# Decoder step of two layers: sample value matmuls alternate between PSUM partition groups, sample vector operations cover both samples, and the inverse subtracts half of the columns

## What is computed

```
kb_all = concat([past_k, kb]); vb_all = concat([past_v, vb])
p = softmax(q . k * 64**-0.5 + forget_bias)
o = einsum('nhqk,nkhd->nqhd', p, v)
```

```
a_mat = where(strict, einsum(kbeta, kc) * decay, 0)
t_mat = triangular_solve(eye + a_mat, eye)
```

## Time and profile before

| | us |
|---|---|
| three runs | 1669.51, 1686.29, 1686.38 |
| profiled execution | 1672.87 |
| its span | 1671.1 |
| PE, DVE busy in the span | 1406.3, 976.6 |
| ACT, POOL busy in the span | 652.9, 217.0 |
| granted PE clock, mean | 0.879 |

### The profile page before, as it was taken

One profiled execution on the slowest core, in us unless ns is written; L12 is line 12 of the kernel. 1 busy time (PEld: TensorE's weight loads), 2 busy tenths in 40 slices (PEclk: granted clock), 3 DMA queues, 4 the chain that ended last, 5 costly groups with the idle time before them and its releaser, 6 DMA issues.

```text
span 1671.1 us, 28028 instructions
## 1 busy us (share of the span) xinstructions
PE 1406.3 (84%) x9968; PEld 1273.6 (76%) x9968; DVE 976.6 (58%) x1596; ACT 652.9 (39%) x1054; POOL 217.0 (13%) x176
## 2 busy tenths in 40 slices
PE   6999979887687478999799999797867775799997
PEld 5999969865465178999799999796645543699996
DVE  4666355575554656664566644657565536566644
ACT  4654443433000245654555544333420002555543
POOL 1000020033222220000110001102231212200000
PEclk9999989957797689999989999897677875899998
DMA  6555645344351243555545646344444302345553
GB/s 212 179 177 159 174 135 169 108 129 133 122 155 54 55 135 120 180 169 158 176 134 184 192 140 189 125 141 125 130 121 144 106 27 81 109 146 181 165 167 95
DMA packets 286120, 234.16 MB, mean 140 GB/s; under 512 B 19899, under 2 KB 282019, under 8 KB 286057
## 3 DMA queue, kind: packets, MB, share of 16 engines
q1 hardware_dynamic: 286056, 233.37, 45.8%
HBM read 228.65 MB, written 5.37 MB: 140 GB/s over the span
## 4 chain that ended last, share of the span: by engine, by line
PE 77%; DVE 16%; ACT 3%; issue 3%; DMA 1%; SPq 0%; DVEq 0%; POOLq 0%; ACTq 0%
PE ps L1396 19%; PE ps L1397 18%; PE ps L1398 18%; PE ps L1591 5%; PE ps L1688 2%; DVE s L1114 1%; PE ps L1687 1%; DVE nlo L937 1%; PE ps L1540 1%; DVE yt L920 1%; PE ps L1543 1%; PE ps L1592 1%; ACT whi L591 1%; PE ps L1509 1%; DVE oms L1153 1%
## 5 line engine op out<-in xcount | busy, mean ns | idle before, releaser
L1396 PE MATMUL ps<-nhi,whi 128*128 128x264 f32 x1936 | 565.1, 292 | 66.9 <-DVE nlo L937 46.3
L1397 PE MATMUL ps<-nlo,whi 128*128 128x264 f32 x1936 | 559.6, 289 | 0.0
L1398 PE MATMUL ps<-nhi,wlo 128*128 128x264 f32 x1936 | 558.8, 289 | 0.0
L888 DVE TENSOR_TENSOR wlo<-raw,whi 128x1024 fp32r<-128x1024 f32 (+2 forms) x376 | 394.6, 1091 | 278.6 <-ACT whi L591 278.3
L1396 PEld LDWEIGHTS ps<-nhi,whi 128*128 128x128 f32 x1936 | 376.4, 194 | 73.5 <-DVE nlo L937 35.0
L591 ACT ACTIVATE whi<-raw 128x1024 fp32r<-128x1024 f32 (+2 forms) x376 | 336.8, 945 | 191.9 <-PE ps L1398 121.7
L1397 PEld LDWEIGHTS ps<-nlo,whi 128*128 128x128 f32 x1936 | 376.5, 194 | 0.2
L1398 PEld LDWEIGHTS ps<-nhi,wlo 128*128 128x128 f32 x1936 | 374.3, 193 | 0.0
L1396 PE MATMUL ps<-hhi,whi 128*128 128x264 f32 x704 | 201.6, 286 | 9.1 <-DVE hlo L905 9.1
L1398 PE MATMUL ps<-hhi,wlo 128*128 128x264 f32 x704 | 200.8, 285 | 0.0
L1397 PE MATMUL ps<-hlo,whi 128*128 128x264 f32 x704 | 200.4, 285 | 0.0
(11 more groups left out here) (337 smaller groups left out, 1645.9 us busy)
## 6 DMA issues: line engine op xcount, KB each, us to landing
raw<-in_ffn_gate_dram SPq DMA_DIRECT2D x44, 1024.0 KB, 5.3
raw<-in_ffn_up_dram SPq DMA_DIRECT2D x44, 1024.0 KB, 5.3
raw<-in_ffn_down_dram SPq DMA_DIRECT2D x64, 704.0 KB, 4.5
raw<-in_w_in_dram SPq DMA_DIRECT2D x24, 1024.0 KB, 5.6
kslot<-in_cache_fox_k_dram SPq DMA_DIRECT2D x128, 128.0 KB, 2.7
vslot<-in_cache_fox_v_dram SPq DMA_DIRECT2D x128, 128.0 KB, 2.4
raw<-in_w_out_dram SPq DMA_DIRECT2D x8, 1024.0 KB, 5.0
kslot<-in_state_swa_k_dram SPq DMA_DIRECT2D x32, 128.0 KB, 2.8
```

Of the source, the lines that this page charges most:

```text
L888: tt2(wlo[s][:, a:b], raw[s][:, a:b], whi[s][:, a:b].bitcast(F32), ALU.subtract).then_inc(S(f"w_lo{s}"), 1)
L1396: mm(out, wh, hi_, start=first, stop=False)
L1397: mm(out, wh, lo_, start=False, stop=False)
L1398: return mm(out, wl, hi_, start=False, stop=last)
```

## The change

Three edits. Line numbers move by up to 7: L1289 and L1290 are L1284 and L1285 after it, L1591 is L1590, L1150 and L1153 are L1147 to L1149.

```
-                        for i in range(2):
-                            b, u = 2 * j + i, 2 * (j % 2) + i
-                            stt(f(s13[:, u, 0:NPG, :]), f(s13[:, u, 0:NPG, :]), sc, f(bias[:, b, 0:NPG, :]), ALU.mult, ALU.add)
+                        two, own = s13[:, u:u + 2, :, :], sx[:, 2 * j:2 * j + 2, :, :]
+                        stt(f(two[:, :, 0:NPG, :]), f(two[:, :, 0:NPG, :]), sc, f(bj[:, :, 0:NPG, :]), ALU.mult, ALU.add)
...
-                            red(pmax[:, i, 0, :], s13[:, u + i, 0:FOX_PG, :].rearrange("p g h -> p h g"), AX.X, ALU.max)
+                        red(pmax[:, :, 0, :], two[:, :, 0:FOX_PG, :].rearrange("p i g h -> p i h g"), AX.X, ALU.max)
...
                     def sample_out(j):
                         dve.wait_ge(S("pv_mm"), V("pv_mm", j + 1))
-                        where = [orow(m, i) for m in range(2) for i in range(2)]
-                        for r0 in where:
-                            ins = dve.reciprocal(small[r0:r0 + H, 124:125], ps[r0:r0 + H, 7, GW:GW + 1])
-                        ch(ins)
-                        for r0 in where:
-                            ins = stt(oms[r0:r0 + H, j, :], ps[r0:r0 + H, 7, 0:GW], small[r0:r0 + H, 124:125],
-                                      const[r0:r0 + H, COL["head_block"][0]:COL["head_block"][0] + GW], ALU.mult, ALU.mult)
-                        ins.then_inc(S("oms"), 1)
+                        den = small[0:OROWS, 124:125]
+                        ch(ts(den, ps[0:OROWS, 7, GW:GW + 1], 0.5, None, ALU.max))
+                        ch(dve.reciprocal(den, den))
+                        stt(oms[:, j, :], ps[0:OROWS, 7, 0:GW], den, C("head_block", OROWS), ALU.mult, ALU.mult).then_inc(S("oms"), 1)
...
+                            part = lambda ap, side: ap.rearrange("p (c a e) -> p c a e", a=2, e=b)[:, :, side, :]
                             if k < len(LEVELS) - 1:
-                                tt2(tm[:, t, :], tm[:, t, :], ps[:, 3 * t + 1, :], ALU.subtract)
-                            tt2(tt[:, t, :], tt[:, t, :], ps[:, 3 * t + 2, :], ALU.subtract).then_inc(S(f"lev{t}"), 1)
+                                tt2(part(tm[:, t, :], 0), part(tm[:, t, :], 0), part(ps[:, 3 * t + 1, :], 0), ALU.subtract)
+                            tt2(part(tt[:, t, :], 1), part(tt[:, t, :], 1), part(ps[:, 3 * t + 2, :], 1), ALU.subtract).then_inc(S(f"lev{t}"), 1)
...
-                            for m, pages, own_page in ((0, range(0, NPG), NPG), (1, range(FOX_PG, FOX_PG + CACHE_T), NPAGE - 1)):
-                                out = ps[orow(m, i):orow(m, i) + H, 7, 0:GW + 1]
-                                for g in pages:
-                                    mm(out, s13[:, u, g, :], vslot[:, i, g - m, :], start=(g == pages[0]), stop=False)
-                                ins = mm(out, s13[0:B, u, own_page, :], v_own[:, m, :], start=False, stop=True)
+                        for g in range(NPG + 1):
+                            for m, own_page in ((0, NPG), (1, CACHE_T)):
+                                if g > own_page:
+                                    continue
+                                for i in range(2):
+                                    u = 2 * (j % 2) + i
+                                    out = ps[orow(m, i):orow(m, i) + H, 7, 0:GW + 1]
+                                    if g < own_page:
+                                        mm(out, s13[:, u, FOX_PG * m + g, :], vslot[:, i, NPG * m + g, :], start=(g == 0), stop=False)
+                                    else:
+                                        ins = mm(out, s13[0:B, u, FOX_PG * m + g, :], v_own[:, m, :], start=False, stop=True)
```

More of the change, by code:

```diff
@@ L1121, in sample_bias @@
                         sc = HD ** -0.5
-                        f = lambda ap: ap.rearrange("p g h -> p (g h)")
-                        for i in range(2):
-                            b, u = 2 * j + i, 2 * (j % 2) + i
-                            stt(f(s13[:, u, 0:NPG, :]), f(s13[:, u, 0:NPG, :]), sc, f(bias[:, b, 0:NPG, :]), ALU.mult, ALU.add)
-                            stt(f(s13[:, u, FOX_PG:FOX_PG + CACHE_T, :]), f(s13[:, u, FOX_PG:FOX_PG + CACHE_T, :]), sc,
-                                f(bias[:, b, NPG:NKT, :]), ALU.mult, ALU.add)
-                        u = 2 * (j % 2)
-                        dve.tensor_copy(s13[:, u:u + 2, NPG, :], sx[:, 2 * j:2 * j + 2, 0, :])
-                        ch(dve.tensor_copy(s13[:, u:u + 2, NPAGE - 1, :], sx[:, 2 * j:2 * j + 2, 1, :]))
-                        for i in range(2):
-                            red(pmax[:, i, 0, :], s13[:, u + i, 0:FOX_PG, :].rearrange("p g h -> p h g"), AX.X, ALU.max)
-                            ins = red(pmax[:, i, 1, :], s13[:, u + i, FOX_PG:NPAGE, :].rearrange("p g h -> p h g"), AX.X, ALU.max)
-                        ins.then_inc(S("s_max"), 1)
+                        f = lambda ap: ap.rearrange("p i g h -> p i (g h)")
+                        u = 2 * (j % 2)
+                        two, own = s13[:, u:u + 2, :, :], sx[:, 2 * j:2 * j + 2, :, :]
+                        bj = bias[:, 2 * j:2 * j + 2, :, :]
+                        stt(f(two[:, :, 0:NPG, :]), f(two[:, :, 0:NPG, :]), sc, f(bj[:, :, 0:NPG, :]), ALU.mult, ALU.add)
+                        stt(f(two[:, :, FOX_PG:FOX_PG + CACHE_T, :]), f(two[:, :, FOX_PG:FOX_PG + CACHE_T, :]), sc,
+                            f(bj[:, :, NPG:NKT, :]), ALU.mult, ALU.add)
+                        dve.tensor_copy(two[:, :, NPG, :], own[:, :, 0, :])
+                        ch(dve.tensor_copy(two[:, :, NPAGE - 1, :], own[:, :, 1, :]))
+                        red(pmax[:, :, 0, :], two[:, :, 0:FOX_PG, :].rearrange("p i g h -> p i h g"), AX.X, ALU.max)
+                        red(pmax[:, :, 1, :], two[:, :, FOX_PG:NPAGE, :].rearrange("p i g h -> p i h g"), AX.X, ALU.max).then_inc(S("s_max"), 1)
                     def sample_shift(j):
@@ L1139, in sample_shift @@
                         dve.wait_ge(S("s_max_all"), V("s_max_all", j + 1))
[L1140 to L1143, removed]
+                        two = s13[:, u:u + 2, :, :]
+                        tt2(two[:, :, 0:FOX_PG, :], two[:, :, 0:FOX_PG, :], pmax_all[:, :, 0, :].unsqueeze(2).broadcast_to([P, 2, FOX_PG, H]), ALU.subtract)
+                        tt2(two[:, :, FOX_PG:NPAGE, :], two[:, :, FOX_PG:NPAGE, :],
+                            pmax_all[:, :, 1, :].unsqueeze(2).broadcast_to([P, 2, SWA_PG, H]), ALU.subtract).then_inc(S("s13"), 1)
                     def sample_out(j):
                         dve.wait_ge(S("pv_mm"), V("pv_mm", j + 1))
-                        where = [orow(m, i) for m in range(2) for i in range(2)]
-                        for r0 in where:
-                            ins = dve.reciprocal(small[r0:r0 + H, 124:125], ps[r0:r0 + H, 7, GW:GW + 1])
-                        ch(ins)
-                        for r0 in where:
-                            ins = stt(oms[r0:r0 + H, j, :], ps[r0:r0 + H, 7, 0:GW], small[r0:r0 + H, 124:125],
-                                      const[r0:r0 + H, COL["head_block"][0]:COL["head_block"][0] + GW], ALU.mult, ALU.mult)
-                        ins.then_inc(S("oms"), 1)
+                        den = small[0:OROWS, 124:125]
+                        ch(ts(den, ps[0:OROWS, 7, GW:GW + 1], 0.5, None, ALU.max))
+                        ch(dve.reciprocal(den, den))
+                        stt(oms[:, j, :], ps[0:OROWS, 7, 0:GW], den, C("head_block", OROWS), ALU.mult, ALU.mult).then_inc(S("oms"), 1)
                     own = v_own[:, 0, 0:GW]
```

1 line of the change is left out of this document (removed).

## The result

The changed kernel took 1600.26 us (median of four: 1603.99, 1597.67, 1602.84, 1590.38), the kernel before on the same chip 1679.22 (median of four, the three runs above and one of 1672.14). The ratio is 0.9547, with a 95% interval from 0.9503 to 0.9591: faster. The profiled execution took 1603.99 us, 68.9 less than the profiled one of before; the sum of the prediction was 67.8 less, 1605.

The account below looks back on a forecast made before the run. PE was taken to bound the value-matmul stretches and DVE what directly follows. Savings of 43.8, 2.2, 14.0, 4.9 and 2.9 sum to 67.8 off 1672.87, so 1605, plus 6 gives 1611 us; range 1592 to 1642.

Parts of the forecast that it names:

- Value matmuls: In `sample_values`, four groups at once: 4.8 us per full-clock call for 12.05; six calls save 43.8, call 0 2.2.
- the calls at half clock: `sample_values` calls starting at half clock keep that time as before: 5.8, 6.7 and 7.4 us, 7.2 to 7.3 off each.
- Vector operations: `sample_out` 0.98 us for 2.73 saves 14.0 over eight calls; fewer instructions in `sample_bias` and `sample_shift` save 2.9.
- Levels: Level subtractions start 0.34 us apart instead of 0.61, gaps costing nothing: 2.43 per layer, 4.9 us in all.
- the cover of PE at full clock: In the levels, PE's products for t = 1 cover the t = 0 subtractions, so only the t = 1 pair counts.
- Rival 3: PE's shorter bursts let the clock fall in the levels: 26 us in levels four to six, 1637; chance 0.08.
- 2 (no overlap): 4-column weights in groups of 32 don't overlap in the value matmuls: about 24.5 us off, 1654; chance 0.10.
- 5 (a drain at each change of group): Each partition-group change empties the array in the value matmuls, nothing overlaps: 23 us slower, 1702; chance 0.03.
- 1: Rival 1: at most two groups at once in the value matmuls, 1.3 us per call, 8 in sum: 1619; chance 0.12.
- Rival 4: A feeder is late (POOL's products, DVE's wait for POOL, a key load): 10 to 20 us, 1625; chance 0.05.
- The 2.38 for three column tiles: Page estimate for the value matmuls: passes 1.26 times as long, six calls 7 us longer, sum 1618.
- The 6 us for the median: Added to 1605 to give 1611; before's four executions had a mean 5.9 us above the profiled one.

Follow-up runs that it names:

- experiment 1: The kernel before with only the value matmuls interleaved, vector operations and levels as before: 1624.92 us, ratio 0.972 to the kernel before.
- experiment 10: The kernel before with the interleaved value matmuls alone, and POOL waiting for the subtraction of the maximum: 1620.87 us, ratio 0.9698.
- experiment 9: The kernel before, with POOL waiting for the subtraction of the maximum before the next pair's product, nothing else: 1669.94 us, ratio 0.9991.
- experiment 11: The kernel before with the both-sample vector operations alone, and POOL waiting for the subtraction of the maximum: 1649.45 us, ratio 0.9871.
- experiment 12: The kernel before with the halved level subtractions alone, and POOL waiting for the subtraction of the maximum: 1662.16 us, ratio 0.9928.
- experiment 3: The kernel before with the halved level subtractions alone: 1663.33 us, ratio 0.9938 to the kernel before.
- experiment 5: The whole change with the 8-row own-row matmuls in one round ahead of the pages: 1595.3 us, ratio 0.9542 to the kernel before.
- experiment 4: The whole change with loops reordered so that never more than two groups run at once: 1602.64 us, ratio 0.9589 to the kernel before.

## Why the prediction was right

**Value matmuls.** Forecast 43.8 and 2.2. Experiments 1 and 10 give 50.0 and 49.1. In experiment 10's profile the mixers are 45.8 us shorter than in experiment 9's (528.6 to 482.8), the forecast 46.0; the stretches that no edit touches vary from 1131 to 1140 us over the profiles, so what the medians have beyond it can't be placed by these two. That the sum came so near is in part luck. The pieces, experiment 10 beside 9: a full clock call took 4.80 (forecast 4.8), and the six calls are 43.1 shorter (43.8). In layer 1 call 0 got 7.3 shorter while the stretch from its end to call 1 grew by 6.2 (26.6 to 32.8), so 1.1 was gained, as forecast; in layer 2 it was 2.1, and in the change itself and in experiment 1 2.8 in each layer. The stages from call 1 to 2 and from 2 to 3 gave back 4.0 in all, which the forecast didn't have, and the stretches ahead of call 0 and behind call 3 gained 3.6, which it had no reason for. The weak piece in the change is the calls at half clock: I gave them the before's time at that clock. The six calls sum to 38.4 us in the change, 41.4 less and not 43.8, because call 1 of both layers stayed longer at half clock (0.68 and 0.52 of full in the windows above).

**Vector operations.** Forecast 14.0 + 2.9 = 16.9; measured 16.8 and 20.5. `sample_out` took 0.87 for 0.98. Beside experiment 9, experiment 11 has the two stages before calls 1 and 2 shorter by 2.5, 3.0, 2.6 and 3.1 us, with one `sample_out`, one bias and one shift in each: forecast 2.24. The stage from call 2 to 3 gives back nearly all (0.3 gained in each layer), by the longer wait in the fifth level: 2.92 us for 1.55.

**Levels.** Forecast 4.9; measured 11.6 and 7.8. The pace of 0.34 us and the 1.1 per layer up to call 2 came true (1.0). For the 1.35 in the later stage the cover of PE at full clock was taken for granted, and it failed. What the medians show beyond this isn't in the levels' own stages, so the size of this term is not settled. The profile of experiment 12 can't settle it: it was the slowest of its eleven runs (1672.03 us, median 1662.16), and its mixers are 3.3 us longer than those of experiment 9 (531.9 for 528.6).

**The half clock.** Rival 3 was right that the clock can fall in the levels, and wrong in the size; its reason isn't borne out. In the change 479.0 to 485.8 ran at 0.52 and cost 2.5 us of the lead; before had the full clock there. Experiments 3, 11 and 12, where the calls still take 12 us, show the same wait in the fifth level (3.17, 2.92, 3.12). So it isn't only the shorter calls that go with the half clock, as the rival said. The twelve layers of the six kernels with one part alone wait 2.75 to 3.28 us there; the four of before and experiment 9 wait 1.55, 2.15, 1.55 and 1.55. But with all three parts it isn't fixed: 3.28 and 1.55 in the two layers of the change, 1.55 and 3.07 in experiment 5. Why the clock falls in one layer and not in the other isn't settled.

**The rivals.** 2 (no overlap) and 5 (a drain at each change of group) are refuted by the 4.80 us call, 1 by the 28 passes in 1.91 us and by experiment 4. Rival 4 expected a late feeder; the timelines of the change name none on the path, and DVE's sum of `sample_add(7)` started at 487.37 with no idle time before it. What the profile had instead was POOL holding DVE, which no step of mine had thought of. By the page "SBUF — State Buffer" of the Trainium skill, section "Who interferes with whom", a DVE instruction with two SBUF inputs contends with a GpSimd instruction that reads SBUF, and the one that issued first holds the ports that they share for its whole length. The trace agrees: 4.28 us beside POOL's 4.50.

**The estimate from the pages.** The 2.38 for three column tiles, which the prediction takes from the page "TensorE: Matmul & The Clock Gate" of the Trainium skill, section "Measured speedup vs the span model", would have made each pass 1.26 times as long and the call about 6 us. The passes stayed at 0.218 with four groups and the call at 4.80, so the measurement decides against carrying it over. The rule of the page "TensorEngine Tiling (Array Packing)" of the Trainium skill, section "Key Properties", that a change of mode drains the engine and a change of tile doesn't, holds on both sides: 0.085 at a change of row height, none to be seen between column groups.

**The 6 us for the median.** They were added because before's median lay above its profiled execution. After, the median is 3.7 below it, and later medians of before were 1670 to 1679. The sum against the profiled execution alone, 1605, was nearer to 1600 than the 1611 I gave.

**Signs and a slip.** Two of the signs that I named failed, and neither changes the cause: the calls after the first took 4.8 to 8.8 us and not 5 to 7.5, and the first call ended 4.4 and 4.1 us before DVE took it, not 6. The prediction also says that DVE does little in seven of the eight calls before; it is six, for call 0 of the second layer is like that of the first (DVE busy for 9.83 of 12.10 us). The sum has call 0 twice, so nothing hangs on it.

## What to carry to other kernels

Small float32 matmuls with four output rows each can go four at once if they write different groups of 32 partitions, even in one bank: count rounds, not matmuls, and put the groups in the inner loop. Put the odd-height ones in one round of their own. Before crediting a shorter DVE step to the end, look whether the PE work behind it had the full clock, and whether PE will still have it: in experiments 3 and 11 the stage with the fifth level gave back nearly all of its gain. Read the room before the next wait in more than one place of the trace: the 1.1 us of call 0 in one layer was 1.7 in the other. When parts are timed alone, compare the stages as well as the medians: the untouched stretches alone vary by 9 us over the profiles.

## What the runs showed of the hardware that was not expected

- Four partition groups of one PSUM bank take float32 matmuls at the same time with no slowing: 28 passes in 1.91 us, starts 7 ns apart.
- A DVE subtraction of two SBUF operands that started 0.31 us behind a POOL product of 2048 columns lasted 4.28 us and not 0.23 (in before 0.12 behind, 4.43 for 0.19). A DVE multiplication of one SBUF tensor by a scalar per partition did so too, 6.64 us for 0.35, in the change's second layer. It started at 1125.75, beside a small POOL instruction, and ended with POOL's two products, which ran from 1125.98 to 1132.24. Each layer of each of the fourteen profiles has one such row, of this form or of `SCALAR_TENSOR_TENSOR`, of 6.63 to 6.71 us, before as after, so it has no part in the difference. Whether it costs the path anything wasn't tried:

```profile
L1058 DVE TENSOR_SCALAR conv_t<-proj,cwt x14: 332/347/6637, 329.0 to 1133.9; 128x256 f32<-128x256 f32 x14
```

- Neither the number of partitions nor gaps between the pieces showed in DVE's time: 0.16 for 100x1 as for 4x1, 0.48 for 100x256 where 4x256 stood 0.49 apart, 0.42 for 128x256 in pieces as in one.
